# Tiles of x and of the output turned by VectorE in 32x32 blocks and moved in runs of 32 numbers, in a fused two-block transformer kernel

## What is computed

```
x = x + gt_x * (concat(oa, ob, oc, od) @ w_out)        # first block: four attention branches
x = x + concat(py, dy) @ even_w_out                    # second block, even layer
x = x + (silu(gate) * o) @ odd_w_out                   # second block, odd layer: the output
```

## Time and profile before

| | |
|---|---|
| median of 3 runs | 2719.26 us (2718.06 to 2721.01) |
| profiled execution | 2719.02 us |
| its span, first to last instruction | 2717.2 us |
| PE busy | 2671.9 us, 98% |
| DVE, ACT, POOL busy | 1137.1, 1005.3, 1262.5 us |
| first output stage, take of tile 0 to take of tile 15 | 1121.55 to 1291.98 us |
| middle output stage, the same | 1873.32 to 2036.52 us |
| last stage, the same | 2541.83 to 2712.27 us |

### The profile page before, as it was taken

One profiled execution on the slowest core, in us unless ns is written; L12 is line 12 of the kernel. 1 busy time (PEld: TensorE's weight loads), 2 busy tenths in 40 slices (PEclk: granted clock), 3 DMA queues, 4 the chain that ended last, 5 costly groups with the idle time before them and its releaser, 6 DMA issues.

```text
span 2717.2 us, 34491 instructions
## 1 busy us (share of the span) xinstructions
PE 2671.9 (98%) x13779; PEld 2147.6 (79%) x13779; DVE 1137.1 (42%) x1889; ACT 1005.3 (37%) x1614; POOL 1262.5 (46%) x655
## 2 busy tenths in 40 slices
PE   7999999999999999999999999999999999999999
PEld 4678988888888777888877778677888887777887
DVE  3257344146540337222123477554223445666311
ACT  4342522342342325322233123664222335666311
POOL 1236135235413537455433445775655555554443
PEclk9999999999999999999999999999999999999999
DMA  9853353136772322544333333324443333223443
GB/s 366 312 183 106 79 167 84 49 88 196 186 121 59 93 63 78 136 116 117 97 88 84 96 88 101 95 72 145 123 116 98 93 93 94 78 78 88 143 116 88
DMA packets 451551, 317.38 MB, mean 117 GB/s; under 512 B 33488, under 2 KB 405968, under 8 KB 448576
## 3 DMA queue, kind: packets, MB, share of 16 engines
q1 hardware_dynamic: 418320, 280.51, 35.4%
q10 hardware_dynamic: 33072, 34.67, 5.3%
HBM read 298.24 MB, written 29.41 MB: 121 GB/s over the span
## 4 chain that ended last, share of the span: by engine, by line
PE 93%; POOL 2%; DVE 1%; issue 1%; ACT 1%; DMA 1%; SPq 1%; DVEq 0%; ACTq 0%; POOLq 0%
PE acc L2240 80%; PE aux L2240 7%; PE ssq L2243 3%; PE ssq L2240 2%; POOL w_lo L1354 1%; PE aux L2243 1%; DMA ada_ring<-in_w_ada 1%; DVE rstd L1709 0%; SPq L766 0%; ACT w_hi L1016 0%; ACT p_t L1167 0%; POOL p L1508 0%; POOL nbr_bias L1424 0%; POOL staged_lo L1371 0%; DVE p L1839 0%
## 5 line engine op out<-in xcount | busy, mean ns | idle before, releaser
L1354 POOL TENSOR_TENSOR w_lo<-raw,w_hi 128x1024 fp32r<-128x1024 f32 x362 | 877.3, 2424 | 1238.2 <-ACT w_hi L1016 1238.2
L2240 PE MATMUL acc<-h_hi,w_hi 128*128 128x512 f32 (+1 forms) x3232 | 1190.5, 385 | 5.2 <-DVE k_t L1721 1.5
L2240 PE MATMUL acc<-h_hi,w_lo 128*128 128x512 f32 (+1 forms) x3232 | 1171.1, 379 | 0.0
L2240 PE MATMUL acc<-h_lo,w_hi 128*128 128x512 f32 (+1 forms) x2464 | 871.5, 376 | 0.0
L1016 ACT ACTIVATE w_hi<-raw 128x1024 fp32r<-128x1024 f32 x362 | 383.8, 1060 | 1028.2 <-PE acc L2240 1004.7
L2240 PEld LDWEIGHTS acc<-h_hi,w_hi 128*128 128x128 f32 x3232 | 583.8, 188 | 150.4 <-issue 34.6
L2240 PEld LDWEIGHTS acc<-h_hi,w_lo 128*128 128x128 f32 x3232 | 583.5, 188 | 117.7
L2240 PEld LDWEIGHTS acc<-h_lo,w_hi 128*128 128x128 f32 x2464 | 439.5, 188 | 82.7 <-issue 1.9
L2240 PE MATMUL acc<-out_t_lo,w_hi 128*128 128x512 f32 x768 | 299.0, 389 | 0.0
L1709 DVE RECIPROCAL rstd<-rstd 128x512 f32<-128x512 f32 (+1 forms) x29 | 118.0, 4071 | 271.1 <-ACT rstd L1068 271.1
L2240 PEld LDWEIGHTS acc<-out_t_lo,w_hi 128*128 128x128 f32 x768 | 144.4, 188 | 28.9
(11 more groups left out here) (306 smaller groups left out, 2636.4 us busy)
## 6 DMA issues: line engine op xcount, KB each, us to landing
raw<-in_w_in SPq DMA_DIRECT2D x52, 1024.0 KB, 5.9
raw<-in_even_w_in SPq DMA_DIRECT2D x41, 1024.0 KB, 5.6
raw<-in_odd_w_in SPq DMA_DIRECT2D x36, 1024.0 KB, 5.6
ada_ring<-in_w_ada SPq DMA_DIRECT2D x32, 1024.0 KB, 6.1
gate_ring<-in_w_ada SPq DMA_DIRECT2D x16, 1024.0 KB, 6.3
raw<-in_w_out SPq DMA_DIRECT2D x16, 1024.0 KB, 5.9
raw<-in_even_w_out SPq DMA_DIRECT2D x16, 1024.0 KB, 5.8
raw<-in_odd_w_out SPq DMA_DIRECT2D x16, 1024.0 KB, 6.6
```

The source lines that it names most:

```text
L1354: G_.tensor_tensor(WL[half][:], RAW[G.rs][:, half * HALF * P:(half + 1) * HALF * P], WH[half][:].bitcast(F32), ALU.subtract).then_inc(S["l ...
L2240: return M.matmul(out_, lhsT, rhs, start=start, stop=stop, skip_group_check=True)
```

## The change

In the first output stage x is now loaded block by block. A column tile is cut in four strips of 32 columns; the DMA of strip a puts it on the partitions 32a to 32a+31, with partition p holding, for each of the 16 blocks of 32 tokens, the 32 columns of token p of that block. A transpose of 32x32 blocks by DVE (`Vv.transpose`, 128x512, from `X` into the buffer `Y`) then gives the turned tile. So a tile takes four DMAs of 64 KB with runs of 32 numbers (128 bytes). SP issues tile 0 and 1 behind the weights of group 1, and tile j behind the weights of group j from then on. `x_turn` on PE and the copy on ACT are gone.

In the last stage DVE makes the same transpose from `FIN` into `FOUT` right behind the add, and the store is four DMAs in runs of 32 numbers. ACT issues all four for tiles 0 to 14; for tile 15 SP issues two and ACT two. `final_turn` on PE and the DVE copy from `AUX` are gone.

```diff
+        def store(eng, G, a):
+            c = G.j * P + 32 * a
+            eng.dma_start(out[0, :, c:c + 32].rearrange("(b p) c -> p b c", p=32),
+                          FOUT[G.js][32 * a:32 * a + 32, :].rearrange("p (b c) -> p b c", c=32))\
+               .then_inc(S[f"out{G.js}"], 16)
 ...
+            def x_blocks(k):
+                need(sp, f"xl{k % 4}", 64 * (k // 4))
+                for a in range(4):
+                    c = k * P + 32 * a
+                    sp.dma_start(ktile(X, k, SEQ)[32 * a:32 * a + 32, :].rearrange("p (b c) -> p b c", c=32),
+                                 T["x"][0, :, c:c + 32].rearrange("(b p) c -> p b c", p=32)).then_inc(S[f"xl{k % 4}"], 16)
 ...
-                    if G.kind in ("wout", "final") and G.j == 1:
-                        sp.wait_ge(S["s_ready"], FIRST_U["d"] + 16) if G.layer == 0 else sp.wait_ge(S["half_done"], 2 * (G.g - 1))
-                        if G.layer == 0:
-                            for k in range(KT):
-                                sp.dma_start(tiles(ktile(X, k, SEQ), QT), T["x"][0, :, k * P:(k + 1) * P]
-                                             .rearrange("(t p) c -> p t c", p=P)).then_inc(S[f"xl{k // 4}"], 16)
+                    if G.kind == "wout" and G.layer == 0 and G.j >= 1:
+                        if G.j == 1:
+                            sp.wait_ge(S["s_ready"], FIRST_U["d"] + 16)
+                            x_blocks(0)
+                        x_blocks(G.j)
 ...
+                sp.wait_ge(S["fin_turned"], KT)
+                for a in (0, 1):
+                    store(sp, G, a)
 ...
                 def send(G):
-                    act.wait_ge(S["fin_copied"], G.j + 1)
-                    act.dma_start(out[0, :, G.j * P:(G.j + 1) * P].rearrange("(t p) c -> p t c", p=P),
-                                  FOUT[G.js][:].rearrange("p (t c) -> p t c", c=P)).then_inc(S[f"out{G.js}"], 16)
+                    act.wait_ge(S["fin_turned"], G.j + 1)
+                    for a in range(4) if G.j < KT - 1 else (2, 3):
+                        store(act, G, a)
 ...
-                    if G.kind == "wout" and G.layer == 0:
-                        act.wait_ge(S["x_turned"], 24 + G.j + 1)
-                        A.activation(ktile(X, G.j, SEQ), AUX[:, 512 * G.js:512 * G.js + 512], ACT.Copy)\
-                         .then_inc(S["x_here"], 1)
 ...
                 def take(G):
                     k, a, j = G.kind, acc(G), G.j
+                    if k == "wout" and G.layer == 0:
+                        dve.wait_ge(S[f"xl{j % 4}"], 64 * (j // 4 + 1))
+                        need(dve, "taken", G.t - 1)
+                        Vv.transpose(Y[G.js][:], ktile(X, j, SEQ)).then_inc(S["x_here"], 1)
                     dve.wait_ge(S["half_done"], 2 * G.g + 2)
 ...
                             e = Vv.scalar_tensor_tensor(out=x, in0=a, scalar=ADA[:, 2 * (GATE_COL + j):2 * (GATE_COL + j) + 1],
-                                                        in1=x, op0=ALU.mult, op1=ALU.add)
+                                                        in1=Y[G.js][:], op0=ALU.mult, op1=ALU.add)
 ...
                         Vv.tensor_tensor(FIN[G.js][:], a, ktile(X, j, SEQ), ALU.add).then_inc(S["taken"], 1)
+                        need(dve, f"out{G.js}", 64 * (j // 2))
+                        dve.wait_ge(S["taken"], G.t + 1)
+                        Vv.transpose(FOUT[G.js][:], FIN[G.js][:]).then_inc(S["fin_turned"], 1)
                         return
 ...
-                    elif k == "final":
-                        dve.wait_ge(S["fin_turned"], G.j + 1)
-                        need(dve, f"out{G.js}", 16 * (G.j // 2))
-                        Vv.tensor_copy(FOUT[G.js][:], AUX[:, 512 * G.js:512 * G.js + 512]).then_inc(S["fin_copied"], 1)
 ...
-                    if k == "final":
-                        final_turn(G)
-                def final_turn(G):
 ...
-                def x_turn(G):
 ...
-                        if k == 11 and G.kind == "wout" and G.layer == 0:
-                            x_turn(G)
 ...
-                final_turn(prev)
```

More of the change, by code:

```diff
@@ L573, in build @@
             "rs_made", "normed", "y_turned", "y_copied", "pooled", "pool_mm", "py_done", "ot_hi", "ot_lo", "sel_done",
-            "fin_turned", "fin_copied",
+            "fin_turned",
             "i_scored", "i_relu", "i_acc",
@@ L841, in late @@
                         sp.dma_start(tiles(raw, KT), src_w(name, c)).then_inc(sem, 16)
-                    if G.kind in ("wout", "final") and G.j == 1:
-                        sp.wait_ge(S["s_ready"], FIRST_U["d"] + 16) if G.layer == 0 else sp.wait_ge(S["half_done"], 2 * (G.g - 1))
-                        if G.layer == 0:
-                            for k in range(KT):
-                                sp.dma_start(tiles(ktile(X, k, SEQ), QT), T["x"][0, :, k * P:(k + 1) * P]
-                                             .rearrange("(t p) c -> p t c", p=P)).then_inc(S[f"xl{k // 4}"], 16)
[L849 to L854, removed]
+                    if G.kind == "wout" and G.layer == 0 and G.j >= 1:
[3 more added lines that the diff above has]
+                        x_blocks(G.j)
+                    if G.kind in ("wout", "final") and G.layer and G.j == 1:
+                        sp.wait_ge(S["half_done"], 2 * (G.g - 1))
+                        sp.wait_ge(S["x_saved"], 256 * G.layer)
+                        for b in range(4):
+                            sp.dma_start(tiles(X, KT, SEQ)[:, 4 * b:4 * b + 4],
+                                         xt_d[G.layer - 1][4 * b:4 * b + 4].rearrange("k p t -> p k t"))\
+                              .then_inc(S[f"xl{b}"], 16)
                     if G.kind == "silu" and G.hooks and G.hooks[0][1] == "dsa":
@@ L1330, in late @@
                 for s in range(2):
-                    act.wait_ge(S[f"out{s}"], 16 * 8)
+                    act.wait_ge(S[f"out{s}"], 64 * 8)
             walk(step, flush, dict(start=start, attend=attend, late=late))
@@ L2079, in take @@
                         x = ktile(X, j, SEQ)
-                        dve.wait_ge(S[f"xl{j // 4}"], 64 + 16 * G.layer)
                         if G.layer == 0:
@@ L2083, in take @@
                             e = Vv.scalar_tensor_tensor(out=x, in0=a, scalar=ADA[:, 2 * (GATE_COL + j):2 * (GATE_COL + j) + 1],
-                                                        in1=x, op0=ALU.mult, op1=ALU.add)
+                                                        in1=Y[G.js][:], op0=ALU.mult, op1=ALU.add)
                         else:
+                            dve.wait_ge(S[f"xl{j // 4}"], 256 + 16 * G.layer)
                             e = Vv.tensor_tensor(x, a, x, ALU.add)
@@ L2091, in take @@
                     if k == "final":
-                        dve.wait_ge(S[f"xl{j // 4}"], 96)
+                        dve.wait_ge(S[f"xl{j // 4}"], 256 + 32)
                         need(dve, "fin_turned", j - 1)
                         Vv.tensor_tensor(FIN[G.js][:], a, ktile(X, j, SEQ), ALU.add).then_inc(S["taken"], 1)
+                        need(dve, f"out{G.js}", 64 * (j // 2))
+                        dve.wait_ge(S["taken"], G.t + 1)
+                        Vv.transpose(FOUT[G.js][:], FIN[G.js][:]).then_inc(S["fin_turned"], 1)
                         return
```

## The result

The changed kernel takes 2705.91 us in the median of four runs (2704.66 to 2706.44). The kernel before, on the same chip, takes 2720.14 (2718.06 to 2722.89). The ratio is 0.9949, 95% interval 0.9937 to 0.9962: faster by 0.5%, 14.2 us between the medians. The forecast was 2704.4 in a range of 2702.6 to 2709.6, a gain of 14.6 to 14.9. The profiled execution took 2705.5 us, with a span of 2703.7 against 2717.2 before: -13.5.

The account below looks back on a forecast made before the run. PE, busy 98% of the span, was taken as the bound. From the profiled 2719.02 us, -7.7 (first stage), -7.2 (last stage) and +0.3 (tail) make -14.6, so 2704.4 us, range 2702.6 to 2709.6.

Parts of the forecast that it names:

- The main term: First and last output stages: without PE transposes, periods fall to the middle stage's 10.88 us, saving 7.7 and 7.2 us.
- The transpose by DVE: First and last output stages: one DVE transpose a tile, 0.6 us, between 0.49 and 1.57, hidden in the periods.
- The short run: Loads and stores of 128-byte runs: 16 ns a run and engine, 2.0 us a tile, DMA engines not binding.
- The first rival: Last-stage stores: a short store costs twice a 512-byte one, 54 ns a run, giving 2709.3 us; chance 10%.
- ACT's issues: Last stage: four store issues a tile instead of one, 4 x 0.38 = 1.5 us, hidden before the next w_hi.
- The tail: From last take to end of span: 0.3 us longer, with bounds of -0.3 to +2.9.
- The rival on the other side: Last stage: dear short runs make it DMA-bound, slower by over 5.4 us from 64 ns a run; chance 6%.
- One stage only: Late first-stage loads, or ACT's four issues delaying w_hi, eat one gain of 7.5 us: 2712 us; chance 6%.
- nothing off PE's path: Changed stages: hand-over PE, ACT, POOL holds the period at 11.36 us, only the tail changes: 2719.3 us; chance 5%.

Follow-up runs that it names:

- e3: Changed kernel with four PE transposes a tile of a constant tile put back in both changed stages, result unread: 2721.88 us, ratio 1.0006.
- e1: Kernel before with only the first output stage's part of the change: 2715.23 us, ratio 0.9983.
- e2: Kernel before with only the last stage's part of the change: 2714.05 us, ratio 0.9976.
- e7: Changed kernel with the first stage's DVE transpose moved behind DVE's wait for the accumulator: 2703.75 us, ratio 0.9929.
- e5b: Changed kernel with last-stage stores cut into 32-byte runs, 16 DMAs a tile: 2764.86 us, ratio 1.0155.
- e6: Changed kernel with all 64 loads of x issued at once at tile 1: 2725.41 us, ratio 1.0008.
- e5: Changed kernel with last-stage stores cut into 64-byte runs, eight DMAs a tile: 2707.90 us, ratio 0.9946.

## Why the prediction was right

**The main term** stood in the trace before: the middle stage as the model of a stage without transposes. 7.7 + 7.2 was forecast; the trace gives 7.2 over 15 periods in each stage, and 0.47 for tile 0 of the first (in the chain of waits, from the last piece ahead of its matmuls to its take: 1111.37 to 1121.55 before, 1112.52 to 1122.23 after). e3 shows that it is the transposes' PE time, e1 and e2 that each stage gives its own share.

**The transpose by DVE** was taken at 0.60 us between 0.49 and 1.57; it takes 0.70 in the first stage and 0.71 in the last. The Trainium skill ("VectorE: DVE Perf Modes", The three transpose paths) gives 311 ns for 128x128 bf16; four of these would have been 1.24 us, an estimate. The trace does not agree with that estimate: four blocks of f32 in one instruction take 0.71; no run here has one of bf16. Its place ahead of the wait was right, and e7 shows that behind the wait it would have been free too.

**The short run** was taken at 16 ns. A store measures 12.0 to 12.8, a load 13 to 16. The first rival, 54 ns, fell. It rested on the Trainium skill ("DMA: Bandwidth & Descriptors", Specifications), by which the engine does a read-modify-write below 512 B. The trace does not show the price of a second pass: down to 32-byte stores the cost of a run only falls, to 8.6 ns. By the byte short runs are dearer all the same: one tile's store takes 1.53 us of the engines, before 0.87.

**ACT's issues** were put at 0.38 us each, 1.5 for four. They take 0.51 in the median, 1.96 for four. SP's, at 0.37 to 1.22 before, take 0.35 to 2.90 for the loads of x, 0.89 in the median, and cost nothing. The prediction laid such long issues to a full queue; e5b and e6 speak against that, since issues late in a long row take 0.51 and 0.49 us and the dear ones lie beside a load of weights. w_hi is still released by PE with 4.38 us of idle before it:

```profile
2678.46 1.96 ACTq L672 DMA_DIRECT2D out<-final_nat  x4
2682.41 1.06 ACT L1033 ACTIVATE w_hi<-raw 128x1024 fp32r<-128x1024 f32 x1 [4.38 <-PE acc L2256]
```

The issues end at 2680.42, 2 us before PE releases it; e5's eight issues fit in 14 of 15 periods, e5b's sixteen do not.

**The tail** was to grow by 0.3 us and grew by 0.1. From the take to the issue it is 1.53 instead of 1.38, by the longer transpose and gaps; from the issue to the end 3.5 instead of 3.9, by the cheaper run.

**The rival on the other side** had the right danger, a last stage held up by small stores, and the wrong resource. I priced the DMA engines, from 64 ns a run; the runs show that ACT's queue gives way first, where sixteen issues fill a period, with the engines half idle over the stage. **One stage only** named that queue and the late loads; e5b and e6 show both dangers real, but beyond what the change does. For **nothing off PE's path** nothing speaks: the hand-over of weights holds at 10.88 in all three stages. The median lies 1.5 us above the forecast, and 0.9 of that is in the kernel before as well: its median of four runs (2720.14) lies 0.9 above the median of three that the prediction had. The gain is 14.2 instead of 14.9. The 0.7 are of the size of the low-clock stretches, which no step of the sum had; that they are the cause is not shown.

## What to carry to other kernels

Where one engine is busy 98% of the span, find a stage in the same trace that already runs without the work in question: the difference of the periods is the price of that work, and needs no model. Then price what takes its place on every queue, not only on the engine that does it: here the transfers were cheap and the number of issues per period, on a queue with a needed operation behind them, was what could have eaten the gain. Spread small transfers over the periods; in one block they cost more than the change brings.

## What the runs showed of the hardware that was not expected

- Short runs are cheap to the engines, a store of 128 bytes 12 ns, 64 bytes 10.2, 32 bytes 8.6, against 27 for 512 bytes. An issue takes 0.38 us for a store of 512 runs of 512 bytes and 0.51 for 512 runs of 128, of 64 or of 32 bytes, so what grows with shorter runs is their number.
- An issue takes 0.51 us also at the end of a row of sixteen (e5b), and 0.49 in the median of 64 in a row (e6), but 0.80 to 1.73 us on ACT's queue while SP's loads of weights move at up to 324 GB/s (e5b).
- In a PE idle of 5.4 us the clock fell to 0.50 a microsecond before its end and stayed there for 6.8 us, so that the idle cost about 3 us more than itself (e5b).
- One and the same h_hi takes 0.49 us or 2.35 us by whether it starts inside an operation of POOL (e7).
- Between executions the clock falls to its lower level at different places (762, 1710, or 30 to 50 us). In e2 the first take came 4.2 us later than before, ahead of any changed code: over half of what one stage of this change brings.
